# Two-layer hybrid encoder trunk: x for the norm in four loads, a later first drain, top-k in smaller pieces, five low parts on GpSimd

## The reference

```python
h = rmsnorm(x, pre_g)
pr = split_columns(einsum('bsd,de->bse', h, w_in))     # 6024 mixer columns and 4 x 2048 gate columns
ya = gmlp_branch(...)          * silu(pr['a_z'])       # spatial gating
yb = mla_branch(...)           * silu(pr['b_z'])       # latent attention, 4 heads
yc = dsa_branch(...)           * silu(pr['c_z'])       # attention over 64 of 256 keys, picked by top-k
yd = swa_sink_branch(...)      * silu(pr['d_z'])       # sliding window with sinks, 8 heads
merged = sum(sigmoid(gate[b]) * (y[b] @ w_branch[b]) for b in range(4))
x = x + rmsnorm(merged @ w_out, post_g)
```

## Time and profile before

| | |
|---|---|
| median of 3 runs | 1721.29 us (1720.52 to 1722.32) |
| profiled execution, its own time | 1721.39 us |
| its span | 1719.6 us |
| PE busy | 1697.5 us, 99% of the span |
| PE weight loads busy | 1410.2 us, 82% |
| DVE busy | 1035.0 us, 60% |
| ACT busy | 777.0 us, 45% |
| GpSimd busy | 182.3 us, 11% |
| DMA | 323.58 MB, mean 188 GB/s |

### The profile page before, as it was taken

How to read it: one execution, slowest core, us unless ns; L and a number is a source line. 1 busy time by engine, 2 the same in 40 slices (tenths; PEclk the granted TensorE clock), 3 DMA queues, 4 the chain that set the end, 5 groups by cost and what they waited for, 6 DMA issues and landing times.

```text
span 1719.6 us, 19969 instructions
## 1 busy us (share of the span) xinstructions
PE 1697.5 (99%) x7926; PEld 1410.2 (82%) x7926; DVE 1035.0 (60%) x1298; ACT 777.0 (45%) x996; POOL 182.3 (11%) x221
## 2 busy tenths in 40 slices
PE   8999999999999999999999999999999999999997
PEld 6888888887888888888788888888788888888886
DVE  6468556666555555555474695655765655554654
ACT  6444444443444444444364434444444444444442
POOL 1020127400000000000010211193000000000000
PEclk9999999999999999999999999999999999999999
DMA  9765575555555766666576655656456556666663
GB/s 321 207 191 179 166 211 158 171 160 184 174 177 150 228 193 192 196 209 207 151 251 195 189 177 176 196 155 176 147 184 194 172 169 208 197 189 193 211 212 113
DMA packets 167261, 323.58 MB, mean 188 GB/s; under 512 B 10304, under 2 KB 62272, under 8 KB 166912
## 3 DMA queue, kind: packets, MB, share of 16 engines
q1 hardware_dynamic: 165152, 315.53, 60.3%
q0 software_dynamic: 1728, 6.50, 1.3%
q10 hardware_dynamic: 288, 0.28, 0.0%
HBM read 318.07 MB, written 4.19 MB: 187 GB/s over the span
## 4 chain that ended last, share of the span: by engine, by line
PE 91%; DVE 5%; DMA 1%; ACT 1%; issue 1%; DVEq 0%; SPq 0%; ACTq 0%
PE ps L1359 29%; PE ps L1361 29%; PE ps L1360 29%; PE ps L1375 3%; DVE w_lo L818 2%; DMA raw<-in_w_in_dram 1%; PE ps L1409 1%; ACT w_hi L494 1%; PE ps L1432 1%; DVE proj L1191 1%; DVE proj L1175 0%; DVE top L1189 0%; ACT area L517 0%; PE ps L1445 0%; DVE wide L924 0%
## 5 line engine op out<-in xcount | busy, mean ns | idle before, releaser
L818 DVE TENSOR_TENSOR w_lo<-raw,w_hi 128x1024 fp32r<-128x1024 f32 (+2 forms) x590 | 733.4, 1253 | 621.5 <-ACT w_hi L494 620.4
L494 ACT ACTIVATE w_hi<-raw 128x1024 fp32r<-128x1024 f32 (+2 forms) x591 | 615.3, 1048 | 823.0 <-PE ps L1361 782.2
L1359 PE MATMUL ps<-w_hi,lhs 128*128 128x512 f32 (+1 forms) x2036 | 796.5, 391 | 6.9 <-DVE w_lo L818 6.9
L1360 PE MATMUL ps<-w_lo,lhs 128*128 128x512 f32 (+1 forms) x2036 | 790.3, 388 | 0.0
L1361 PE MATMUL ps<-w_hi,lhs 128*128 128x512 f32 (+1 forms) x2036 | 790.3, 388 | 0.0
L1359 PEld LDWEIGHTS ps<-w_hi,lhs 128*128 128x128 f32 x2036 | 382.5, 188 | 88.4 <-DVE w_lo L818 7.1
L1361 PEld LDWEIGHTS ps<-w_hi,lhs 128*128 128x128 f32 x2036 | 382.5, 188 | 77.6
L1360 PEld LDWEIGHTS ps<-w_lo,lhs 128*128 128x128 f32 x2036 | 382.8, 188 | 75.0
L1359 PE MATMUL ps<-w_hi,yT 128*128 128x512 f32 (+1 forms) x304 | 116.7, 384 | 0.0
L1361 PE MATMUL ps<-w_hi,yT 128*128 128x512 f32 (+1 forms) x304 | 116.6, 383 | 0.0
L1360 PE MATMUL ps<-w_lo,yT 128*128 128x512 f32 (+1 forms) x304 | 116.5, 383 | 0.0
(11 more groups left out here) (181 smaller groups left out, 742.3 us busy)
## 6 DMA issues: line engine op xcount, KB each, us to landing
raw<-in_w_in_dram SPq DMA_DIRECT2D x256, 512.0 KB, 4.3
raw<-in_w_in_dram SPq DMA_DIRECT2D x191, 502.0 KB, 4.4
raw<-in_w_branch_dram SPq DMA_DIRECT2D x64, 512.0 KB, 3.7
raw<-in_w_out_dram SPq DMA_DIRECT2D x64, 512.0 KB, 4.4
raw<-in_b_w_uq_dram SPq DMA_DIRECT2D x8, 384.0 KB, 3.3
wide<-in_x_dram SPq DMA_DIRECT2D x2, 1024.0 KB, 8.4
raw<-in_b_w_ukv_dram SPq DMA_DIRECT2D x8, 256.0 KB, 2.7
proj<-in_post_norm_g_dram POOLq DMA_DIRECT2D x2, 1024.0 KB, 5.8
```

The source lines that it names most:

```text
L494: act.activation(wslot(w_hi, s, n), wslot(raw, s, n), ACT.Copy).then_inc(hi_done, 1)
L818: dve.tensor_tensor(wslot(w_lo, s, n), wslot(raw, s, n), wslot(w_hi, s, n).bitcast(F32), ALU.subtract).then_inc(lo_done, 1)
L1359: pe.matmul(o, hi, wh[:, k], start=a, stop=False)
L1360: pe.matmul(o, hi, wl[:, k], start=False, stop=False)
```

## The change

1. **x for the norm** comes in four loads of 512 KB, one ahead of each of the chunks 9, 10, 11, 12, in place of two of 1 MB ahead of chunk 9. ACT squares each behind the high part of chunk 9, 10, 11 and 12. The first drain (and norm) moves behind chunk 13 (ACT) and behind 12 and 13 with norm between them (DVE).
2. **The first loads**: SyncE waits for the first half of chunk 0's weights before it issues xT piece 2 and chunk 2, and for the second half before piece 3 and chunk 3.
3. **Group 11**: PE does six chunks, not four, ahead of `turn_prob`. In G = 0, ACT and DVE split chunks 104 and 105 ahead of the copies `B5`.
4. **Top-k**: tile 0's eight rounds run as 4 + 4, behind chunks 130 and 132; tile 1's run as 2 + 2 + 2 + 2 in place of 3 + 3 + 2, the first two behind chunk 135.
5. **Five low parts per layer** (chunks 130, 132, 134, 136, 139, `POOL_LO`) are made by GpSimd, in its list behind the last rotation, with a semaphore of their own (`pool_lo`); all who wait for a low part do so through `lo_seen`.

```diff
+POOL_LO = [GATE0 + 2 * CG + 6, GATE0 + 2 * CG + 8, GATE0 + 3 * CG, GATE0 + 3 * CG + 2, GATE0 + 3 * CG + 5]
-        ss = sb("ss", [P, TT, 2])
+        ss = sb("ss", [P, TT, NG])
+        def lo_seen(eng, l, j):
+            by_pool = l * len(POOL_LO) + len([i for i in POOL_LO if i <= j])
+            if j in POOL_LO:
+                eng.wait_ge(pool_lo, by_pool)
+            else:
+                eng.wait_ge(lo_done, l * CHUNKS + j + 1 - by_pool)
...
                                 if c > 0:
+                                    if c == 2:
+                                        sp.wait_ge(first_loaded, 16)
+                                    if c == 3:
+                                        sp.wait_ge(raw_loaded[0], 16)
                                     load_xT(c)
...
-                            if l == 0 and g0 == 0 and g == 1 and c == 1:
-                                for i in range(2):
-                                    w = slice(i * D_MODEL // 2, (i + 1) * D_MODEL // 2)
-                                    sp.dma_start(wide[:, :, w], x[0].rearrange("(t p) d -> p t d", p=P)[:, :, w]).then_inc(x_loaded[i], 16)
+                            if l == 0 and g0 == 0 and g == 1 and 1 <= c < 5:
+                                w = slice((c - 1) * NW, c * NW)
+                                sp.dma_start(wide[:, :, w], x[0].rearrange("(t p) d -> p t d", p=P)[:, :, w]).then_inc(x_loaded[c - 1], 16)
...
@@ GpSimd, behind the rotation "d"
+                pool.wait_ge(pool_s.sem, pool_s.at(l, "d"))
+                for j in POOL_LO:
+                    n, s = w_shape(j), j % SLOTS
+                    pool.wait_ge(hi_done, l * CHUNKS + j + 1)
+                    pool.tensor_tensor(wslot(w_lo, s, n), wslot(raw, s, n), wslot(w_hi, s, n).bitcast(F32),
+                                       ALU.subtract).then_inc(pool_lo, 1)
...
@@ ACT, groups 1 to 4
-                    splits(l, j, j + 2)
                     if l == 0 and g == 1:
-                        act.wait_ge(x_loaded[0], 16)
-                        squares(0, slice(0, D_MODEL // 2))
-                    splits(l, j + 2, j + 3)
-                    if l == 0 and g == 1:
-                        act.wait_ge(x_loaded[1], 16)
-                        squares(1, slice(D_MODEL // 2, D_MODEL)).then_inc(*act_s.did("ss"))
-                    splits(l, j + 3, j + 4)
+                        splits(l, j, j + 1)
+                        for i in range(NG):
+                            splits(l, j + 1 + i, j + 2 + i)
+                            act.wait_ge(x_loaded[i], 16)
+                            last = squares(i, slice(i * NW, (i + 1) * NW))
+                        last.then_inc(*act_s.did("ss"))
+                        splits(l, j + 5, j + 6)
+                    else:
+                        splits(l, j, j + 4)
                     act.wait_ge(dve_s.sem, dve_s.at(l, "rn"))
                     drain(l, g - 1, proj[:, 0, (g - 1) * MW:g * MW], j - 1, rn[:, 0:1])
-                    splits(l, j + 4, j + CPG)
+                    splits(l, j + (6 if l == 0 and g == 1 else 4), j + CPG)
...
@@ DVE, groups 1 to 4
                     splits(l, j, j + 4)
                     if l == 0 and g == 1:
+                        splits(l, j + 4, j + 5)
                         norm()
+                        splits(l, j + 5, j + 6)
                     dve.wait_ge(dve_s.sem, dve_s.at(l, "rn"))
                     drain(l, g - 1, proj[:, 1, (g - 1) * MW:g * MW], j - 1, rn[:, 1:2])
...
@@ DVE, gate groups
                     splits(l, j, j + 1)
-                    if G == 3:
-                        select("sel1", 1, 0, 3)
...
+                    if G == 3:
+                        splits(l, j + 1, j + 2)
+                        select("sel1", 1, 0, 2)
+                        splits(l, j + 2, j + 4)
+                        select("sel1", 1, 2, 4)
...
                     if G == 3:
-                        select("sel1", 1, 3, 6)
+                        select("sel1", 1, 4, 6)
...
-                    splits(l, j + 5, j + 8)
+                    if G == 2:
+                        splits(l, j + 5, j + 7)
+                        select("sel0", 0, 0, 4)
+                        splits(l, j + 7, j + 8)
+                        select("sel0", 0, 4, 8)
+                    else:
+                        splits(l, j + 5, j + 8)
...
@@ PE, groups 9 to 11
-                    chunks(l, j, lhs, MW, b0, 0, 4)
+                    cut = 6 if g == 11 else 4
+                    chunks(l, j, lhs, MW, b0, 0, cut)
```

More of the change, by code:

```diff
@@ L166, in trunk @@
         hi_done, lo_done, mm_done = sem("hi_done"), sem("lo_done"), sem("mm_done")
+        pool_lo = sem("pool_lo")
         act_drained, dve_drained = sem("act_drained"), sem("dve_drained")
@@ L170, in trunk @@
         xt_loaded = [sem(f"xt_loaded{c}") for c in range(CPG)]
-        x_loaded = [sem(f"x_loaded{i}") for i in range(2)]
+        x_loaded = [sem(f"x_loaded{i}") for i in range(NG)]
         first_x, first_loaded, first_hi, warm = sem("first_x"), sem("first_loaded"), sem("first_hi"), sem("warm")
@@ L266, in load @@
             def load(l, j, slot, src):
-                if l > 0 or j >= SLOTS:
-                    sp.wait_ge(lo_done, l * CHUNKS + j + 1)
+                if j >= SLOTS:
+                    lo_seen(sp, l, j - SLOTS)
+                elif l > 0:
+                    lo_seen(sp, l - 1, CHUNKS + j - SLOTS)
                 sp.dma_start(wslot(raw, slot, src.shape[1:]), src).then_inc(raw_loaded[slot], 16)
@@ L674, in _ @@
                     j = GATE0 + G * CG
-                    splits(l, j, j + 1)
+                    splits(l, j, j + (2 if G == 0 else 1))
                     if G == 0:
@@ L815, in split @@
                 jn = j if jn is None else jn
+                if j in POOL_LO:
+                    return
                 n, s = w_shape(jn), jn % SLOTS
@@ L960, in norm @@
                     dve.wait_ge(act_s.sem, act_s.at(l, "ss"))
-                    link(dve.tensor_reduce(ms[:, 0:TT], ss[:], AX_X, ALU.add))
+                    link(dve.tensor_reduce(ms[:, 0:TT], ss[:, :, 0:NG if l == 0 else 2], AX_X, ALU.add))
                     link(dve.tensor_scalar(ms[:, 0:TT], ms[:, 0:TT], 1.0 / D_MODEL, EPS, ALU.mult, ALU.add))
@@ L986, in _ @@
                     stream(1)
-                    dve.wait_ge(lo_done, l * CHUNKS + 1 + SLOTS)
+                    lo_seen(dve, l, 0)
                     splits(l, 1, 3)
@@ L1218, in _ @@
                         dve.reciprocal(rinv[:, :, 0:4], sums[:, :, 0:4])
+                        splits(l, j + 1, j + 2)
                         dve.wait_ge(pe_s.sem, pe_s.at(l, "B5"))
                         dve.tensor_copy(probT[:, 512:1024], bank(5)).then_inc(*dve_s.did("B5"))
-                    splits(l, j + 1, j + 4)
+                    if G == 3:
+                        splits(l, j + 1, j + 2)
+                        select("sel1", 1, 0, 2)
+                        splits(l, j + 2, j + 4)
+                        select("sel1", 1, 2, 4)
+                    else:
+                        splits(l, j + (2 if G == 0 else 1), j + 4)
                     if G == 0:
@@ L1254, in _ @@
                         gated("D6b", 1, 4)
-                    splits(l, j + 5, j + 8)
+                    if G == 2:
[3 more added lines that the diff above has]
+                        select("sel0", 0, 4, 8)
+                    else:
+                        splits(l, j + 5, j + 8)
                     if G == 0:
                         times_silu("zC", "c_z")
-                    if G == 2:
-                        select("sel0", 0, 0, 8)
                     if G == 3:
@@ L1351, in chunk @@
                 s = jn % SLOTS
-                pe.wait_ge(lo_done, l * CHUNKS + j + 1 + SLOTS)
+                lo_seen(pe, l, j)
                 wh, wl = wslot(w_hi, s, (nk, n)), wslot(w_lo, s, (nk, n))
@@ L1479, in _ @@
                         for k in range(KC):
-                            seen(dve_s, "hT0a") if k == 0 else pe.wait_ge(lo_done, 1 + SLOTS)
+                            seen(dve_s, "hT0a") if k == 0 else lo_seen(pe, 0, 0)
                             n = w_shape(0)[1]
@@ L1583, in _ @@
                         turn_prob(1, B_HEADS, 5, 512).then_inc(*pe_s.did("B5"))
-                    chunks(l, j, lhs, MW, b0, 4, CPG)
+                    chunks(l, j, lhs, MW, b0, cut, CPG)
                 for G in range(GATES):
@@ L1723, in _ @@
                         c = CPG - 1
-                        pe.wait_ge(lo_done, (l + 1) * CHUNKS + SLOTS)
+                        lo_seen(pe, l, CHUNKS - 1)
                         wh, wl = (wslot(w, (j + c) % SLOTS, (KC, NW)) for w in (w_hi, w_lo))
```

2 lines of the change are left out of this document (removed).

## The result

The changed kernel takes 1713.05 us (median of 5 runs, 1712.17 to 1713.53) where the kernel before, timed beside it, takes 1720.52 (5 runs, 1719.37 to 1722.32). The ratio is 0.9951, 95% interval 0.9937 to 0.9965: faster, by half a per cent. The profiled execution took 1713.53 us, its span is 1711.7; before, the two were 1721.39 and 1719.6.

A forecast was written before the change was run, and what follows sets the result against it. PE's standstills and lower-clock stretches were taken as all that can be shortened. Gains of 0.8 + 3.9 + 2 x 0.4 + 2 x 1.5 = 8.5 us gave a median of 1712.8 us, range 1710.3 to 1716.3.

The forecast's parts named there:

- What bounds the kernel: Whole kernel: PE is busy 1697.5 of 1719.6 us, so only its standstills or lower-clock stretches can be shortened.
- First loads, +0.8: Start of chunk 1: holding back chunks 2 and 3 lands its weights sooner, 0.8 us won.
- rival B: First loads: holding back gives nothing, as the rings are in order; 1713.6 us, 17%.
- x and chunk 12, +3.9: Before chunk 12: smaller x loads and later norm remove 2.2 us idle and 1.7 of low clock, 3.9 us.
- Cut in group 11, 2 x 0.4: Group 11: chunks 100 and 101 ahead of prob's transposes shorten PE's wait for softmax, 0.4 us per layer.
- Top-k, 2 x 1.5: Chunk 135: its low part ahead of top-k's rounds, and GpSimd's low parts, end PE's wait; 1.5 us per layer.
- Sum: Whole kernel: 0.8 + 3.9 + 2 x 0.4 + 2 x 1.5 = 8.5 us won.
- The boundary: Layer boundary: 2.8 us idle and a low-clock stretch left untouched, the stretch may go or stay; 0.6 us possible gain.
- C: Top-k stretch: contention keeps PE waiting at chunk 135 or 138; 3.0 us more, 1715.8 us, 13%.
- D: First loads: holding back starves chunks 2 and 3, -0.8 in place of +0.8; 1714.4 us, 6%.
- E: Chunk 12: x still lands too late, or the clock falls anyway; 1.7 to 3.9 us more, 1715.6 us, 4%.
- F: Top-k stretch: GpSimd's low parts block top-k's rounds too, PE loses up to 5.6 us per layer; slower, 1727 us, 4%.

The follow-up runs named there:

- run 2: Kernel before with only the two waits that hold back the first loads added: 1719.04 us in one profiled execution.
- run 3: Kernel before with only x in four loads and the later norm and drain: 1715.79 us in one profiled execution.
- run 4: Kernel before with only x in four loads and the later norm and drain, timed in several executions: 1716.80 us, ratio 0.9978.
- run 7: Changed kernel with all low parts on VectorE, none on GpSimd: 1713.29 us in one profiled execution.
- run 12: Kernel before, unchanged, profiled once more: 1721.09 us.
- run 5: Changed kernel without the two waits that hold back the first loads, timed in several executions: 1713.67 us, ratio 0.9962.
- run 8: Changed kernel with the old order of top-k's rounds, GpSimd's low parts kept: 1724.56 us in one profiled execution.
- run 6: Changed kernel with PE's cut in group 11 back at 4: 1714.02 us in one profiled execution.
- seven fillers: Changed kernel with seven instead of four matmuls of unread result at the end of layer 1: 1712.35 us profiled; median 1713.15 us, ratio 0.9958.

## Why the prediction was right

The forecast for the median was 1712.8 us with a range of 1710.3 to 1716.3; measured 1713.05. For the profiled execution it was 1712.9; measured 1713.53. That the median came within 0.3 us is in part luck: the forecast counted down from a median of 1721.29, and beside the changed kernel the one before had 1720.52, so the gain itself was 7.5 where 8.5 was forecast. By its steps:

- **What bounds the kernel.** Right: behind chunk 2 every step of the lead over 0.06 us stands at one of the places that PE's waits named, or at chunk 138 (0.13). VectorE is loaded as before, and the time moved only where PE had stood.
- **First loads, +0.8.** The profile of after shows 0.92 at chunk 1 and 0.62 behind chunk 2, which would confirm it, were it not that the landing differs by over a microsecond between executions without the hold. Over fourteen profiles it is 0.55. The direction is likely, the size was too high by a third, and one pair of profiles could not have shown it. The mechanism, held transfers that no longer share the DMA engines with chunk 1, is not shown. By the Trainium skill (DMA: Bandwidth & Descriptors, Queues, rings and completion order) descriptors are consumed in ring order; by that chunk 1's bytes were ahead anyway and the term would be near 0 (rival B). The averages speak against that, the overlap of the two groups keeps it from being settled.
- **x and chunk 12, +3.9.** Right: 3.99 between 30 and 100 us in the changed kernel, as alone in two profiles, and 3.78 alone in the median. The cause was right too, as far as runs 2 to 4 go: chunk 12's low part hung on x and norm and not on PE. Whether it was the 2 MB of x or norm's place ahead of it is not shown. This term is half of the whole gain.
- **Cut in group 11, 2 x 0.4.** Right: 0.44 right behind the group and 0.39 further on, in both layers, and as much is lost when it is undone; the gap that is left loses 0.37 where 0.3 to 0.4 was expected.
- **Top-k, 2 x 1.5.** The size is right (1.53 and 1.43: 1.56 at chunk 135 in each layer, less 0.03 and 0.13 at chunk 138), the share of GpSimd in it is not: run 7 has all of it with nothing on GpSimd. The contention was priced at up to 2.2 us, twice, and came as 2.14 (5.75 against 3.61) and 2.20 (3.42 against 1.22). The low part of 135 was to end between 385.6 and 390.0. It ended at 385.06, since I left out of these absolute times that the whole stretch would run 5 us earlier; on the old kernel's times it is 385.06 + 5.04 = 390.10, the late end of that range. Counted from PE's need it was 0.56 early: with nothing on GpSimd it is some 3.8 us early (381.62 in run 7), so the two blocked instructions used up nearly all the slack that the new order had won. That the rounds of top-k would not be blocked is right: of the rounds that run beside a low part on GpSimd no `MAX8` or `MATCH_REPLACE8` in the trace of after takes longer than 0.43 us. By the Trainium skill (GPSIMD Engine Reference, Specifications) it is instructions in a 2-port mode or with two SBUF inputs that contend. The trace agrees on the second: the score (5.75 in place of 3.61) and the low part (3.42 in place of 1.22) have two, and the rounds, of one, keep to 0.43. No run here shows a 2-port mode.
- **Sum.** Predicted 8.5; between the two profiles 7.86. The four terms are 0.62 + 3.99 + 0.78 + 2.96 = 8.35, less 0.55 at the boundary: 7.8. The medians differ by 7.5. Three of the terms are as fixed as the edits: 3.99, 0.39 per layer and 1.56 per layer come out the same to 0.03 us in every profile that has them. What moves between profiles is the front (a lead of -0.14 to 0.92 at 30 us), the boundary (-0.73 to +0.61) and chunk 138.
- **The boundary.** I left it as it was, with 0.6 as a possible gain. It came out as a loss of 0.55, and the 0.6 is there in the profiles with the full level (0.59 to 0.61). The step behind this fails: "Idles of 1.90 and 1.27 left the clock at full level, 2.07 and 2.76 did not" holds in the one profile and not in the next. Idles of 2.68 and 2.76 left it at full level in runs 2 and 12. In the eleven profiles with the boundary's unfilled pause of some 2.8 to 3.0 us the low level followed in seven and stayed away in four. It followed in all six of the changed kernel and its variants and in one of the five others, so it may not be chance alone; no run shows what in the change would do it. Against a full level it costs 0.6 us where it starts half a microsecond ahead of the transposes (before, runs 5 and 8) and 1.2 where it starts 0.5 or 1.6 us behind them (after, run 6).

Of the rivals, C (contention keeps PE waiting) happens at chunk 138 in some executions, worth up to 1.5 us and not 3. Of D (chunks 2 and 3 starved) there is 0.3 us at chunk 2 in the profile of after, 0.2 in that of run 7 and nothing in the six others with the hold. E (x too late, or the clock falls anyway) shows in none of the eleven profiles with the new x loads. F (slower) needed top-k's rounds themselves to be blocked, which they are not; yet run 8, with the old order, ends at 1724.6 by F's neighbour: the score is blocked twice, 4.3 us, and PE's gap with the low clock behind it costs 6.2 us in layer 1. With the old order of the rounds GpSimd's low parts make the kernel slower than before in spite of the other edits: 1724.56 against 1722.00 in one execution of each on the same chip.

Still open: why the landing of chunk 1 moves between 7.6 and 8.7 us without the hold, what decides whether the level falls behind a pause of 2 to 3 us, and how much of the 1.2 us at the boundary, which all three profiles with seven fillers keep at a full level, a median would show beside the changed kernel with nothing on GpSimd.

## What to carry to other kernels

- Where the tensor engine is busy 99%, list its waits by place and end each by order: a low part ahead of top-k's rounds, a load cut and a norm moved so that the low part behind them is not late. That gave 1.5 per layer and 3.8 us.
- Work moved to GpSimd is not free for VectorE. A VectorE instruction with two SBUF inputs that meets such an instruction (2.4 us here) ends about when it would have ended had it begun at GpSimd's end: it cost 0.5 to 2.2 us a time here. Try the new order without the move first.
- A term under 1 us at a DMA landing or a clock stretch can't be read from one pair of profiles. Profile the unchanged kernel again first, and look at several profiles.

## What was not expected of the hardware

- The clock's low stretches are by execution as much as by pause: after the same 2.76 us of idle at the boundary the granted clock was 0.5 in one profile of the kernel before and 1.00 in the other.
- A GpSimd instruction that starts 0.06 us ahead of a VectorE low part holds it until about its own end: 3.42 us in place of 1.22. Started 0.34 ahead it cost 1.92 (3.14). Started 1.02 us sooner it cost 0.95 (2.17), and PE lost 0.5 in place of 1.5.
- Chunk 1's weights, issued at the same place in the queue, were split first at 7.61 us in one profile and at 8.69 in another of kernels whose first loads are the same.
